# FFN1 pairs: the modulation chunks move from VectorE to GpSimd, and the round ends one pair later

## The reference

```
m_lat = (silu(c)     @ ada_w + ada_b).reshape(b, 9, 1, d)
m_ctx = (silu(c_ctx) @ ada_w + ada_b).reshape(1, 9, 1, d)
x   = x   + 0.5 * m_lat[:, 2] * swiglu(modulate(rms_norm(x,   norm1_g), m_lat[:, 0], m_lat[:, 1]), ffn1_w_in, ffn1_w_out)
ctx = ctx + 0.5 * m_ctx[:, 2] * swiglu(modulate(rms_norm(ctx, norm1_g), m_ctx[:, 0], m_ctx[:, 1]), ffn1_w_in, ffn1_w_out)
...   # retention and latent attention, gated by m_lat[:, 5], then a second FFN with m_lat[:, 6..8]
```

## Time and profile before

| | |
|---|---|
| time, median of 3 | 2681.8 us |
| the profiled execution | 2683.84 us, of which span 2682.0 us |
| TensorE busy | 2632.7 us, 98% |
| VectorE busy | 2134.1 us, 80% |
| ScalarE busy | 1216.8 us, 45% |
| GpSimd busy | 93.7 us, 3% |
| HBM read, written | 505.22 MB, 13.63 MB |

### The profile page before, as it was taken

How to read it: one execution, slowest core, us unless ns; L and a number is a source line. 1 busy time by engine, 2 the same in 40 slices (tenths; PEclk the granted TensorE clock), 3 DMA queues, 4 the chain that set the end, 5 groups by cost and what they waited for, 6 DMA issues and landing times.

```text
span 2682.0 us, 37985 instructions
## 1 busy us (share of the span) xinstructions
PE 2632.7 (98%) x15293; PEld 2327.4 (87%) x15293; DVE 2134.1 (80%) x2328; ACT 1216.8 (45%) x1399; POOL 93.7 (3%) x131
## 2 busy tenths in 40 slices
PE   5999999999999999999999999999999999999998
PEld 4778999999999998888888988888988888888887
DVE  6869878788787877899797877586688888888866
ACT  6642344444444443231175543465465455555543
POOL 0000111111111110000000000000000000000000
PEclk9999999999999999999999999999999999999999
DMA  9967699999999888667584585442455555556463
GB/s 309 295 199 211 182 245 249 230 249 250 231 232 258 231 232 289 210 226 243 187 279 135 137 263 189 136 132 79 141 177 194 194 194 197 203 204 206 168 220 125
DMA packets 428939, 558.71 MB, mean 208 GB/s; under 512 B 22274, under 2 KB 280696, under 8 KB 428024
## 3 DMA queue, kind: packets, MB, share of 16 engines
q1 hardware_dynamic: 414156, 504.64, 58.4%
q0 software_dynamic: 14384, 51.92, 10.0%
q10 hardware_dynamic: 252, 0.10, 0.0%
HBM read 505.22 MB, written 13.63 MB: 193 GB/s over the span
## 4 chain that ended last, share of the span: by engine, by line
PE 87%; DVE 4%; ACT 1%; issue 1%; DMA 0%; ACTq 0%; DVEq 0%
PE py L1538 14%; PE py L1540 14%; PE py L1539 14%; PE pg L1538 3%; PE pg L1539 3%; PE pg L1540 3%; PE py L2071 3%; PE py L2073 3%; PE py L2072 3%; PE two L2013 2%; PE two L2015 2%; PE two L2014 2%; PE pu L2052 1%; PE pu L2054 1%; PE pu L2053 1%; PE pu L1538 1%
## 5 line engine op out<-in xcount | busy, mean ns | idle before, releaser
L2455 DVE TENSOR_TENSOR wl<-raw,wh 128x1024 fp32r<-128x1024 f32 x252 | 307.8, 1222 | 111.7 <-ACT wh L1045 111.5
L1045 ACT ACTIVATE wh<-raw 128x1024 fp32r<-128x1024 f32 x252 | 265.7, 1055 | 288.7 <-DVE raw L2459 228.0
L2176 DVE TENSOR_TENSOR wl<-raw,wh 128x2048 fp32r<-128x2048 f32 x101 | 231.1, 2288 | 124.4 <-ACT wh L902 124.2
L1538 PE MATMUL py<-ah,wh 128*128 128x512 f32 (+1 forms) x720 | 277.2, 385 | 0.3 <-issue 0.3
L1539 PE MATMUL py<-al,wh 128*128 128x512 f32 (+1 forms) x720 | 276.8, 384 | 0.0
L1540 PE MATMUL py<-ah,wl 128*128 128x512 f32 (+1 forms) x720 | 276.8, 384 | 0.0
L902 ACT ACTIVATE wh<-raw 128x2048 fp32r<-128x2048 f32 x100 | 190.7, 1912 | 189.0 <-PE py L1540 84.6
L1538 PE MATMUL py<-hh,wh 128*128 128x256 f32 (+1 forms) x752 | 226.1, 301 | 1.8 <-DVE hl L2253 1.0
L1539 PE MATMUL py<-hl,wh 128*128 128x256 f32 (+1 forms) x752 | 224.8, 299 | 0.0
L1540 PE MATMUL py<-hh,wl 128*128 128x256 f32 (+1 forms) x752 | 224.8, 299 | 0.0
L1538 PE MATMUL py<-fhs,wh 128*128 128x256 f32 x720 | 204.0, 283 | 0.4 <-DVE wl L2455 0.4
(11 more groups left out here) (516 smaller groups left out, 7124.9 us busy)
## 6 DMA issues: line engine op xcount, KB each, us to landing
raw<-in_ffn_w_out SPq DMA_DIRECT2D x84, 1024.0 KB, 5.2
chunk<-in_ada_w SPq DMA_DIRECT2D x160, 512.0 KB, 5.5
raw<-in_ffn_w_in SPq DMA_DIRECT2D x144, 512.0 KB, 7.5
raw<-in_ffn_w_in SPq DMA_DIRECT2D x58, 1024.0 KB, 5.1
sraw<-in_ffn_w_in SPq DMA_DIRECT2D x40, 1024.0 KB, 5.1
raw<-raw POOLq DMA_DIRECT2D x72, 512.0 KB, 5.8
raw<-in_ada_w SPq DMA_DIRECT2D x64, 512.0 KB
raw<-in_mix_w_in SPq DMA_DIRECT2D x30, 1024.0 KB
```

Of the source, the lines that this page charges most:

```text
L1045: nc.scalar.activation(wh[:, slot, o:o + 1024], s_half(k, S_SRC[name]), ACT.Copy).then_inc(wh_ready, 1)
L1538: mm(out_ap, w[0], xh_ap, start=first, stop=False, skip_group_check=True)
L2176: tt(wl[:, slot % 2, :], raw[:, slot, :], wh[:, slot % 2, :].bitcast(F32), ALU.subtract).then_inc(wl_ready, 1)
L2455: tt(wl[:, slot, o:o + 1024], s_half(k, S_SRC[forms(k)[pos]]), wh[:, slot, o:o + 1024].bitcast(F32), ALU.subtract).then_inc(wl_ready, 1)
```

## The change

GpSimd's loop over the pairs gets `chunk_step(c)` for the chunks of `S_CHUNKS`, behind the sums of pair k and the store of pair k-1. The first chunk of a round is one multiplication into `accl`; every other one is a multiplication of the chunk in place by its column of scalars, a wait for it (`pool_chain`, a semaphore that an earlier stage has left at BLOCKS = 8), and an addition to `accl`. VectorE's loop loses the chunk steps. Its turn, reduction and total of a round that ended in pair k - 1 stand in pair k: the turn behind `gate_lat(k-1)`, the reduction behind the low half of the fifth product, the total behind that of the sixth. The last round's end stands behind `down_low(1)`, past the stage. The chunks' loads and their buffers stay, and so does the split of the chunks over the pairs.

```diff
@@ -365,6 +365,7 @@
     p7_summed, p4_summed = far_loaded, nfb_loaded
+    pool_chain, POOL0 = rows_turned, BLOCKS
@@ -866,9 +867,24 @@
             for k in range(FIRST_S - 1):
                 act_store(k)
+            def chunk_step(c):
+                t = c % KT
+                pool.wait_ge(chunk_loaded[SIGNAL[c]], CHUNK_BASE[SIGNAL[c]] + 16 * LOADS[c])
+                pool.wait_ge(chunk_free, c + 1)
+                if t == 0:
+                    pool.wait_ge(sums_ready, (TAKEN[c // KT] - 1) * 5 + 1)
+                    ins = nc.gpsimd.tensor_scalar(accl[:], chunks[PLACES[c]], cs[:, 0, 0:1], None, ALU.mult)
+                else:
+                    nc.gpsimd.tensor_scalar(chunks[PLACES[c]], chunks[PLACES[c]], cs[:, t, 0:1], None, ALU.mult).then_inc(pool_chain, 1)
+                    pool.wait_ge(pool_chain, POOL0 + c - KT + 1 - c // KT)
+                    ins = nc.gpsimd.tensor_tensor(accl[:], accl[:], chunks[PLACES[c]], ALU.add)
+                ins.then_inc(chunk_free, 1)
+
             for k in range(FIRST_S, PAIRS):
                 sums_added(k)
                 act_store(k - 1)
+                for c in S_CHUNKS[k - FIRST_S]:
+                    chunk_step(c)
             act_store(PAIRS - 1)
@@ -2503,32 +2519,17 @@
                     gate_lat(k - 1)
-                    for c_ in span[:-3]:
-                        chunk_step(c_)
+                    for c_ in S_CHUNKS[k - FIRST_S - 1]:
                         if ends_round(c_):
                             take_turn(c_, 0)
                     half_low(k, 2)
-                    for c_ in span[:-3]:
-                        if ends_round(c_):
-                            take_reduce(c_, 0)
                     half_low(k, 3)
                     pair_gate(k - 1)
-                    for c_ in span[:-3]:
-                        if ends_round(c_):
-                            take_total(c_, 0)
-                    for n, c_ in enumerate(span[-3:]):
-                        chunk_step(c_)
-                        if ends_round(c_):
-                            take_turn(c_, 0)
+                    for n in range(3):
                         half_low(k, 4 + n)
-                        if ends_round(c_):
-                            take_reduce(c_, 0)
-                        if n and ends_round(c_ - 1):
-                            take_total(c_ - 1, 0)
-                    for n in range(len(span), 3):
-                        half_low(k, 4 + n)
-                    if ends_round(span[-1]):
-                        take_total(span[-1], 0)
+                        for c_ in S_CHUNKS[k - FIRST_S - 1]:
+                            if ends_round(c_) and n < 2:
+                                (take_reduce, take_total)[n](c_, 0)
                 up_lat(k)
@@ -2547,6 +2548,11 @@
             down_low(1)
+            for c_ in S_CHUNKS[-1]:
+                if ends_round(c_):
+                    take_turn(c_, 0)
+                    take_reduce(c_, 0)
+                    take_total(c_, 0)
```

## The result

The changed kernel takes 2832.0 us (median of 4, 2829.6 to 2837.3) against 2682.0 us: a ratio of 1.056, 95% interval 1.054 to 1.058, so +150 us. That is slower, as forecast, but by two and a half times the +61 us that the forecast had, and outside its range.

What follows compares the result with a forecast made beforehand. TensorE, busy 98% of the span, was taken as the bound. Exclusion +49 us and round ends +12 us gave +61 us on the profiled 2683.8 us, 2745, or 2743 us for the median; range 2682 to 2796.

Steps and rivals of the forecast that it cites:

- VectorE's relief: Chunk steps leaving VectorE, some 120 us: hidden behind TensorE, worth 0 to 2.5 us, taken as 0.
- the moved round ends: Turn, reduction and total one pair later, the last behind down_low(1): cost 0.
- The addition: GpSimd's addition of two 128x1024 tensors: taken at 2.2 us, between 1.81 and 2.66.
- The term for exclusion: GpSimd's and VectorE's SBUF reads in the pairs shut each other out: +53.3 us less 3.9 in hand, +49 us.
- the forecast's own chain: Pair length under exclusion, block, P7 sum, then w_sum to gate: 22.87 us with three chunks, 18.25 with two.
- the price of the multiplication: GpSimd's multiplication of a 128x1024 chunk: taken at 1.0 us, between 0.95 and 1.81.
- the upper bounds of both prices together: Multiplication at 1.81 and addition at 2.66 us: pairs of 26.7 and 20.8 us, +171 us.
- Three chunks alone: GpSimd's block between store and P7 sum: 10.2 us fits its idle 11.61 us, ending at 627.5.
- the P7 sum's last moment: Latest issue of P7's accumulating DMA, counted back from P7's start: 635.8, 6.9 us after its issue at 628.93.
- Round ends: Four inner round ends inside a pair's chunks, GpSimd waiting for VectorE's turn: 3 us each, 12 us, 0 to 20.
- Rival 3: GpSimd near 1.8 and 2.7 us and more, with exclusion, its own chain the bound: 2796 to 2870 us, chance 0.06.
- the memset's 0.83 ns a column: GpSimd's price per column from memset rows, with 0.10 us fixed: one pass of 1024 columns 0.95 us.

Runs made afterwards that it cites:

- E11: Kernel before, all chunks still on VectorE, with rounds that end with pairs and the round ends one pair later: 2685.4 us, ratio 1.0011.
- E1: A kernel of its own without the layer, short series of 128x1024 instructions alone and beside other engines: GpSimd's multiplication 2.84 us alone, addition 2.34 us; no kernel time compared.
- E6: Changed kernel with both accumulating DMAs and the stage's chunk loads left out, rounds ending with pairs, GpSimd's arithmetic kept: 2735.2 us, ratio 1.020.
- E5: Changed kernel with GpSimd's arithmetic replaced by memsets, six for a chunk, three for a round's first: 2785.7 us, ratio 1.038.
- E9: E3 with ScalarE's copy of P5's result moved ahead of P7's high part: 2823.2 us, ratio 1.053 against the kernel before.
- E3: Changed kernel with the chunks split over the pairs so that every round ends with a pair: 2815.5 us, ratio 1.049.
- E7: Changed kernel without GpSimd's multiplications except each round's first, the change's own split of chunks kept: 2719.1 us, ratio 1.014.
- E10: E7 with rounds that end with pairs: 2692.6 us, ratio 1.0038 against the kernel before.
- E8: Changed kernel with the third chunk of each pair worked on only in its first 8 columns: 2777.4 us, ratio 1.035.

## Why the prediction was wrong

**Where it was right.** TensorE set the end, VectorE's relief was worth nothing, and the moved round ends cost nothing that shows (E11). The addition was taken at 2.2 us and takes 2.34 alone. The exclusion is there: VectorE's 1.22 us becomes 2.84 beside additions, and 1.58 beside multiplications (E1). The Trainium skill (SBUF — State Buffer, "Who interferes with whom") says that a VectorE instruction with two inputs from SBUF contends with a GpSimd instruction that reads SBUF; E1 agrees for both, and with multiplications what it shows is milder than full blocking. The Trainium skill's length of an addition of 2048 columns (GPSIMD Engine Reference, § 3.1), halved to an estimate of 2.25 us, is close to the 2.34 of E1.

**Where the number was luck.** The term for exclusion, +49 us, lies near E6's +53, but E6 has GpSimd's real prices. With E1's 2.84 and 2.34 us in place of 1.0 and 2.2 the forecast's own chain gives 28.8 us for a pair with three chunks and 22.2 with two, some +240 us, where E6 has 22.0 and 19.8. So the term came out by two errors against each other: a price too low, and an exclusion taken as full that comes near to it only with additions.

**The step that failed: the price of the multiplication.** "I take 1.0, since a read and a write need not share a path", with 1.81 as the upper bound, both drawn from a memset. It takes 2.84 us alone and 3.47 beside VectorE. A memset writes and does no arithmetic; it was the nearest row, and not near. The upper bound should have been as open as the row was far. And the forecast had worked out +171 us for the upper bounds of both prices together, and left that out of its range, which would then have held the result. At 1.0 us a chunk came to 3.4 us; it is 5.4 alone with its hand-overs, 6.4 in the kernel.

**What hung on it.** "Three chunks alone take 10.2 us, to 627.5: they fit." With 6.4 us they take 19.2, from 617.3 to 636.5, past the P7 sum's last moment of 635.8; and its landing takes 7.0 us (median after) and not the 6.0 of the earlier trace rows, which brings that moment to 634.8. So the P7 sum is late again and again (22 of 36 leave right behind GpSimd's other work, and TensorE stops 17 times), where the prediction had it late at two round ends. By the lone 5.4 us a chunk the block would end at 633.5, in time by this deadline though not by the one of the next paragraph, so exclusion's lengthening has a part in it. E5 puts a block of 6.1 us a chunk at 103.5 us with the round ends. The text had the queue right ("What is queued behind them is the P7 sum") and, having found that the block fitted, gave it no term.

**The deadline itself was set too late.** It was counted back from P7's start. The wait shows before P3, by the copy that stands behind P7's high part in ScalarE's list, and not on VectorE's low parts of P6 or P5, where the prediction looked for it. P3 starts 2.88 us before P7 and the copy takes 0.37 us instead of the low part's 1.22, so the limit was some 2 us tighter (an estimate from these rows). E9 shows that this link is no cause of its own: with the copy moved the wait is for P7's low part.

**A term that was missing: TensorE's clock.** After a stop the matmuls run at the lower clock for a while, and 36 of the 150 us are that. The prediction priced waits only.

**Round ends** were put at 12 us (0 to 20) and cost 16.5 in the changed kernel (E3) and 26.5 where nothing else is late (E7 against E10). **Rival 3** (GpSimd dearer, 2796 to 2870) is what came by its price and its number, and it had 0.06; its mechanism, GpSimd's own chain as the bound, holds only in part, since GpSimd was busy 642 of the stage's 881 us and 14 of its 36 P7 sums still waited for VectorE. The argument against it, the memset's 0.83 ns a column, was the same far row once more.

Not settled: what the multiplication alone would cost in this place, what two chunks a pair would without a leftover third, and how the 150 us divide between the block's own length and what exclusion adds to it.

## What to carry to other kernels

Before work moves to an idle engine, look at what that engine's queue carries besides: GpSimd was 3% busy, and one of its three DMA issues a pair, the P7 sum, was soon on the path of the products. A price for an operation that no row shows should be open upward until it is measured; one short kernel (E1) gives it, alone and beside the other engine. And an engine that is busy 99% of a stage can only lose from a change beside it, so that such a change needs a reason other than the time of that stage.

## What the runs showed of the hardware

GpSimd's multiplication of 128x1024 by a column takes 2.84 us and its addition of two tensors 2.34, the cheaper although it reads twice as much; with a constant in place of the column four take 11.32 us, against 11.64 with it. Right behind the issue of an accumulating DMA they take 3.16 and 2.64 us. Of the 24 multiplications of 8 columns in E8, 3 took 0.31 us, 11 took 1.09 and 10 took 2.14 to 2.16: the shortest show that there is little fixed cost, and the others are longer beside VectorE's work (the one of 2.14 us above ends at 490.64, a weight sum of VectorE at 490.54). ScalarE's copies beside them changed neither. VectorE's one-tensor multiplication, 0.75 us alone, took 1.16 us on average beside GpSimd's multiplications and 2.32 beside its additions, so leaving out the second tensor did not spare it; in the instruction with one tensor from PSUM and one from SBUF no hindrance shows, on either engine.
